# The last three units' rows by products with 0/1 matrices, and the last normed tile from its features

## The chip, the cores and the metric

The kernel runs on one core of a Trainium2 chip. The metric is device time in microseconds, from the first to the last instruction with what lies around it; lower is better. Five engines run their own queues: PE (TensorE, matmuls), DVE (VectorE), ACT (ScalarE), POOL (GpSimd) and SP (SyncE, which here only issues DMAs). They meet at semaphores.

## What is computed

One layer of an encoder for 512 tokens of width 1024, in float32: norm and one input projection, two branches (a chunked gated delta rule and a sliding-window attention), their gated merge, an output projection, then a hierarchical mixture of experts and a final norm. The part that the change touches most:

```python
def hierarchical_moe(h, w_rg, b_rg, w_re, b_re, w_gate, w_up, w_down):
    # top-1 group of 4, then top-2 of its 4 experts; weight = p_group * softmax(top-2 logits)
    ...
    for gi in range(N_EXPERT_GROUPS):
        e = slice(gi * EXPERTS_PER_GROUP, (gi + 1) * EXPERTS_PER_GROUP)
        act = jax.nn.silu(jnp.einsum('td,edf->tef', t, w_gate[e])) * jnp.einsum('td,edf->tef', t, w_up[e])
        out = out + jnp.einsum('tef,efd->td', act * combine[:, e, None], w_down[e])
...
x = x + hierarchical_moe(rms_norm(x, norm_ffn_w[layer]), ...)
return rms_norm(x, norm_final_w)
```

## The kernel before

Every float32 operand of a large product is split into a high part (rounded, on ACT) and a low part (the rest, on DVE), and `three` (L1582 to L1584) makes one product out of three matmuls: hi x hi, lo x hi, hi x lo. All matmuls of this kind have line 1582, 1583 or 1584.

**Start.** Four tiles of x (128 tokens each) are squared and rooted on ACT, scaled on DVE (L1046, L1047) and turned on PE into features (L1594). Ahead of that stands a turn of the small vectors (`small_rows`, 65 of them, L1588), which DVE copies to `small_cols` (L1041) before it scales x. The input projection follows, and in it a product for beta and decay with 8 columns of weights, 24 matmuls, and its turn (L1610).

**Routing.** After the output projection the residual sum y is turned, 20 router logits per token come from `residual_logits` (L1907), and DVE works out each token's group, its two experts (L1409 to L1444) and its place in the expert's list. Meanwhile the rows of the FFN input are written to HBM (`ffn_rows`, L598): tiles 0 to 2 normed by DVE, tile 3 scaled by ACT (L968) and multiplied by the norm's weights by POOL (L718). While PE waits it repeats a product 20 times (`keep_busy`, L1943) ahead of the rank product (L1949).

**Experts.** A unit is one expert with up to 128 of its tokens. There are 23: the 16 experts and 7 extra units for experts with more tokens, in the order of `SEQ`; numbers 4, 7, 10, 13, 16, 19 and 21 are extra ones. Their weights are gathered by POOL with computed row numbers (L703); those of the others are loaded by SP (L588). For unit u POOL gathers the tokens' rows (`fetch`, L688), PE turns them (L1983), makes gate and up, turns the hidden values (L1999) and multiplies them by the down weights; ACT copies the result to `unit_out` (L988), and POOL scatters it to `expert_rows_hbm` (`spread`, L711). Each engine writes its own loop by hand; in pass u DVE does in this order: hidden of u-1, low part of the gate weights of u+1, of the tokens of u+1 (`unit_in_lo`, L1501), of the down weights of u-1 (L1351), of the hidden values of u-1 (L1547), of the up weights of u+1. PE does in pass u: turns of u+1, first half of gate/up of u, turn of hidden u-1, second half, down of u-1.

**Tail.** When the last rows are in HBM, SP loads two rows per token back (`expert_rows`, L611), DVE adds them to y with the weights of the two choices (L1561, L1562), ACT squares and roots, DVE norms (L1568, L1569), SP stores each tile.

## Time and profile before

| | |
|---|---|
| time, median of 3 runs (lowest, highest) | 700.14 us (698.49, 701.82) |
| the profiled execution: time / span | 698.2 us / 696.5 us |
| PE busy | 644.4 us, 93% of the span |
| DVE busy | 473.3 us, 68% |
| ACT busy | 394.0 us, 57% |
| POOL busy | 176.3 us, 25% |
| chain of work that ended last, by engine | PE 83%, DVE 7%, DMA 3% |

The table gives shares over the whole. In most of the span PE is the engine that works without a pause, and the others wait for it; at the two ends and in the routing it is the other way round. So what an edit is worth has to be read at its place, from the timeline there: which engine idles in front of an instruction, and what released it.

### The profile page before, as it was taken

How to read it: one execution, taken by the hardware profiler on the slowest of the kernel's cores; microseconds unless marked ns; L12 is line 12 of the kernel's file. 1: busy time of each engine (PE TensorE's matmuls, PEld its weight loads, DVE VectorE, ACT ScalarE, POOL GpSimd, SP SyncE). 2: the span in 40 equal slices, each digit the busy share in tenths (PEclk: the TensorE clock that was granted, in tenths of full speed). 3: DMA queues.
4: the chain of work that ended last, by engine and by line, in shares of the span. 5: the costliest groups of instructions: out<-in, count | busy, mean ns of one | idle time of the engine just before them, and what ended most of it. 6: DMA issues, size and time to landing. Idle time of an engine off the chain costs nothing.

```text
span 696.5 us, 9239 instructions
## 1 busy us (share of the span) xinstructions
PE 644.4 (93%) x3371; PEld 535.8 (77%) x3372; DVE 473.3 (68%) x779; ACT 394.0 (57%) x664; POOL 176.3 (25%) x217
## 2 busy tenths in 40 slices
PE   5999999999999999999999998899999999999910
PEld 4688788788878888888888885788878888887810
DVE  4778995265521434425665549899999999998717
ACT  6449583355624233243432443388898898987623
POOL 7000009981000000000000002145545546455210
PEclk9999999999999999999999997699999999999975
DMA  8524343213222222113235615468787797866335
GB/s 270 178 67 96 61 106 121 62 60 76 66 61 62 61 61 60 62 61 95 88 121 223 260 62 191 164 196 287 216 272 249 224 313 240 292 225 216 104 140 241
DMA packets 73729, 104.63 MB, mean 150 GB/s; under 512 B 31634, under 2 KB 53203, under 8 KB 73555
## 3 DMA queue, kind: packets, MB, share of 16 engines
q1 hardware_dynamic: 60912, 95.57, 42.3%
q0 software_dynamic: 12672, 8.43, 4.0%
q8 instruction: 27, 0.44, 0.3%
q14 instruction: 20, 0.16, 0.1%
q10 hardware_dynamic: 98, 0.03, 0.0%
HBM read 123.90 MB, written 17.83 MB: 203 GB/s over the span
## 4 chain that ended last, share of the span: by engine, by line
PE 83%; DVE 7%; DMA 3%; ACT 2%; POOL 2%; issue 2%; SPq 0%; POOLq 0%; ACTq 0%; DVEq 0%
PE bank L1582 22%; PE bank L1584 22%; PE bank L1583 22%; PE bank L1983 2%; PE bank L1718 2%; PE bank L1907 1%; PE bank L1628 1%; DVE down_lo L1351 1%; DMA expert_rows<-expert_rows_hbm 1%; PE bank L1787 1%; PE bank L1777 1%; PE bank L1737 1%; DMA ew_raw<-in_w_down,extra_weight_rows 1%; PE bank L1750 1%; DVE rank_onehot L1466 1%
## 5 line engine op out<-in xcount | busy, mean ns | idle before, releaser
L1582 PE MATMUL bank<-h_hi,w_hi 128*128 128x512 f32 x304 | 123.1, 405 | 1.0 <-POOL index_row_i L662 1.0
L1584 PE MATMUL bank<-h_hi,w_lo 128*128 128x512 f32 x304 | 118.7, 390 | 0.0
L1583 PE MATMUL bank<-h_lo,w_hi 128*128 128x512 f32 x304 | 118.5, 390 | 0.0
L1351 DVE TENSOR_TENSOR gate_up_lo<-ew_raw,gate_up_hi 128x1024 fp32r<-128x1024 f32 x92 | 108.3, 1219 | 10.6 <-ACT gate_up_hi L950 8.4
L950 ACT ACTIVATE gate_up_hi<-ew_raw 128x1024 fp32r<-128x1024 f32 x92 | 92.2, 1056 | 9.1 <-DMA ew_raw<-in_w_gate,extra_weight_rows 7.8
L1037 DVE TENSOR_TENSOR w_lo<-w_raw,w_hi 128x2048 fp32r<-128x2048 f32 x26 | 60.2, 2317 | 50.1 <-ACT w_hi L744 50.0
L1582 PE MATMUL bank<-gate_up_hi,unit_in_hi 128*128 128x512 f32 x184 | 76.7, 417 | 0.0
L1584 PE MATMUL bank<-gate_up_hi,unit_in_lo 128*128 128x512 f32 x184 | 72.9, 396 | 0.0
L1583 PE MATMUL bank<-gate_up_lo,unit_in_hi 128*128 128x512 f32 x184 | 72.6, 394 | 0.0
L718 POOL TENSOR_TENSOR ffn_in_T<-ffn_in_T,norm_ffn_b 128x1024 f32<-128x1024 f32 x1 | 2.3, 2346 | 261.5 <-ACT ffn_in_T L968 261.5
L1582 PEld LDWEIGHTS bank<-h_hi,w_hi 128*128 128x128 f32 x304 | 57.2, 188 | 12.3 <-issue 1.5
L1584 PEld LDWEIGHTS bank<-h_hi,w_lo 128*128 128x128 f32 x304 | 57.1, 188 | 12.2
L1583 PEld LDWEIGHTS bank<-h_lo,w_hi 128*128 128x128 f32 x304 | 57.3, 188 | 10.5 <-issue 0.2
L744 ACT ACTIVATE w_hi<-w_raw 128x2048 fp32r<-128x2048 f32 x26 | 49.7, 1910 | 16.0 <-PE bank L1584 16.0
L1351 DVE TENSOR_TENSOR down_lo<-ew_raw,down_hi 128x1024 fp32r<-128x1024 f32 x44 | 52.0, 1222 | 6.1 <-ACT down_hi L950 4.4
L711 POOL DMA_INDIRECT expert_rows_hbm<-unit_out,row_index x23 | 25.2, 1095 | 84.3 <-DVE gate_up_lo L1351 49.7
L674 POOL TENSOR_TENSOR sub_product<-sub_low,sub_inv 128x496 f32<-128x496 f32 (+30 forms) x31 | 22.6, 730 | 89.5 <-DMA sub_low<-chunk_low_hbm 87.2
L950 ACT ACTIVATE down_hi<-ew_raw 128x1024 fp32r<-128x1024 f32 x44 | 44.5, 1072 | 0.8 <-DMA ew_raw<-in_w_down,extra_weight_rows 0.7
L1584 PEld LDWEIGHTS bank<-gate_up_hi,unit_in_lo 128*128 128x128 f32 x184 | 35.0, 190 | 7.9
L688 POOL DMA_INDIRECT unit_tokens<-ffn_rows,row_index x23 | 30.6, 1332 | 38.1 <-DVE row_index L1474 24.3
L1582 PEld LDWEIGHTS bank<-gate_up_hi,unit_in_hi 128*128 128x128 f32 x184 | 35.4, 192 | 6.0
L1583 PEld LDWEIGHTS bank<-gate_up_lo,unit_in_hi 128*128 128x128 f32 x184 | 35.2, 192 | 6.1
(361 smaller groups left out, 1335.8 us busy)
## 6 DMA issues: line engine op xcount, KB each, us to landing
w_raw<-in_w_in SPq DMA_DIRECT2D x17, 1024.0 KB, 5.2
ew_raw<-in_w_gate SPq DMA_DIRECT2D x32, 512.0 KB
ew_raw<-in_w_up SPq DMA_DIRECT2D x32, 512.0 KB
ew_raw<-in_w_down SPq DMA_DIRECT2D x32, 512.0 KB
w_raw<-in_w_out SPq DMA_DIRECT2D x4, 1024.0 KB, 5.0
expert_rows<-expert_rows_hbm SPq DMA_DIRECT2D x8, 512.0 KB, 7.3
x_T<-in_x SPq DMA_DIRECT2D x4, 512.0 KB, 4.9
w_raw<-in_w_in SPq DMA_DIRECT2D x8, 256.0 KB, 4.2
```

Source lines behind the costliest of these rows:

```text
L674: link(nc.gpsimd.tensor_tensor(sub_t[:, j + 1:, :], sub_l[:, j + 1:, j:j + 1].broadcast_to(w), sub_x[:, j:j + 1, :].broadcast_to(w), ALU.m ...
L688: nc.gpsimd.indirect_dma_start(out=xg[u % 2][:, :], out_offset=None, in_=h_rows[:, :], in_offset=bass.IndirectOffsetOnAxis(ap=ridx[:, c, 1 ...
L711: nc.gpsimd.indirect_dma_start(out=o_rows[:, :], out_offset=bass.IndirectOffsetOnAxis(ap=ridx[:, SEQ[u], 0:1], axis=0), in_=ot[u % 2][:, : ...
L744: act.activation(whi[u % RING][:, :], raw[u % RING][:, :], ACT.Copy).then_inc(hi_done, 1)
L950: act.activation(dst[half], eraw[slot][:, :], ACT.Copy).then_inc(ehi_done, 1)
L1037: dve.tensor_tensor(wlo[s][:, :], raw[s][:, :], whi[s][:, :].bitcast(F32), ALU.subtract).then_inc(lo_done, 1)
L1351: dve.tensor_tensor(dst, eraw[slot][:, :], hi.bitcast(F32), ALU.subtract).then_inc(elo_done, 1)
L1582: pe.matmul(out_ap, lhs_hi, rhs_hi, start=first, stop=False)
L1583: pe.matmul(out_ap, lhs_hi, rhs_lo, start=False, stop=False)
L1584: return pe.matmul(out_ap, lhs_lo, rhs_hi, start=False, stop=last)
L1718: ins = pe.matmul(o, qb[d, h, m * P:(m + 1) * P], kb[d, m * P - P + c0:(m + 1) * P], start=True, stop=True)
L1983: ins = pe.transpose(bank4(2 + k // 4)[:, k % 4, :], xg[u % 2][:, :].rearrange("p (c k) -> p k c", k=KT)[:, k, :], ident[:, :])
```

## The change

Six edits go in together.

1. The turns of x start before the small rows are turned; DVE copies `small_cols` after it has scaled two tiles.
2. The hi and lo weights of beta/decay stand side by side, 16 columns in one tile, and two matmuls per step (hi|lo with h_hi, hi with h_lo) replace three. The turn adds the two halves with small products.
3. The last tile of the FFN input comes from the turned residual: ACT multiplies its features by the norm's weights (`last_features`), PE turns them back (8 turns), ACT scales by the rms factor. POOL's multiply is gone. 12 repeated products stand where 20 did.
4. Unit 1's turns go to banks 5 and 4 and wait for the row numbers alone, no longer for `unit_in_lo` of unit 0.
5. The last three units (20, 21, 22; `LATE`) are not scattered to HBM. Their down product is weighted and split into hi and lo (`late_out_hi` on ACT, `late_out_lo` on DVE), and PE multiplies it by a 0/1 matrix of 128 tokens by 128 rows, per tile and unit, which adds every row to its token (`late_rows`). What is needed for it: 0/1 matrices made by DVE in pass 6 (`late_onehots`), weights of the rows, which SP writes out as a table (8 small stores) and POOL gathers in pass 12 (3 gathers of 128x1), and zeros in `expert_rows_hbm` from 16 stores early on, since rows of late units are no longer written there.
6. The rows of the other units are loaded back when unit 19 is out, and the tail adds them (`add_pair`) and the products (`add_late`) in an order written out by hand. The first add stands in DVE's pass 22, in front of the late split of unit 20.

The core of the diff:

```diff
-            dve.wait_ge(rows_ps, 1)
-            dve.tensor_copy(cols[:, :], ps[7][:, 0:65]).then_inc(cols_done, 1)
             for t in range(TT):
+                if t == 2:
+                    dve.wait_ge(rows_ps, 1)
+                    dve.tensor_copy(cols[:, :], ps[7][:, 0:65]).then_inc(cols_done, 1)
...
-                    ins = three(ps[4][0:8, :], ba_hi[:, k, :], ba_lo[:, k, :], h_hi[:, k, :], h_lo[:, k, :],
-                                k == 0, k == KT - 1)
+                    pe.matmul(ps[4][0:16, :], ba_hl[:, k, :], h_hi[:, k, :], start=k == 0, stop=False)
+                    ins = pe.matmul(ps[4][0:8, :], ba_hi[:, k, :], h_lo[:, k, :], start=False, stop=k == KT - 1)
...
+                if 4 <= u < 8:
+                    for r_ in range(2 * (u - 4), 2 * (u - 4) + 2):
+                        for half in range(2):
+                            sp.dma_start(o_rows[P * r_:P * (r_ + 1), S * half:S * (half + 1)],
+                                         sub_t[:, :, :].rearrange("p i c -> p (i c)")).then_inc(zero_rows, 16)
...
-            pool.wait_ge(choice_exp, ROW_SCALED)
-            pool.wait_ge(x2_in, 80)
-            nc.gpsimd.tensor_tensor(tx[:, TT - 1, :], tx[:, TT - 1, :], nffn[:, :], ALU.mult).then_inc(pool_set, 1)
...
+            pe.wait_ge(hf_act, TT + 1)
+            for k in range(KT):
+                ins = pe.transpose(bank4(2 + k // 4)[:, k % 4, :], last_f[:, k, :], ident[:, :])
+            ins.then_inc(tt_ps, 1)
-            keep_busy(20)
+            keep_busy(12)
...
-                if u:
+                if u == 1:
+                    pe.wait_ge(ids_done, 4)
+                elif u:
                     pe.wait_ge(xs_lo_done, u)
...
-                spread(u)
+                if u < LATE[0]:
+                    spread(u)
+                if u == 12:
+                    pool.wait_ge(wt_out, 16 * 2 * TT)
+                    pool.wait_ge(ids_done, EARLY + 4)
+                    for i, v in enumerate(LATE):
+                        nc.gpsimd.indirect_dma_start(
+                            out=l_w[:, i:i + 1], out_offset=None, in_=wt_rows[:, :],
+                            in_offset=bass.IndirectOffsetOnAxis(ap=ridx[:, SEQ[v], 0:1], axis=0),
+                            bounds_check=2 * S - 1, oob_is_err=False).then_inc(wt_in, 16)
...
-            sp.wait_ge(ot_out[(UNITS - 2) % 2], 16 * ((UNITS - 2) // 2 + 1))
-            sp.wait_ge(ot_out[(UNITS - 1) % 2], 16 * ((UNITS - 1) // 2 + 1))
-            sp.wait_ge(gu_ps, UNITS)
+            for i in range(2):
+                u = LATE[0] - 1 - i
+                sp.wait_ge(ot_out[u % 2], 16 * (u // 2 + 1))
...
+            def late_out_lo(i):
+                dve.wait_ge(xt_ps, (UNITS - 1, UNITS, UNITS)[i])
+                for h in range(2):
+                    hs = slice(S * h, S * (h + 1))
+                    dve.wait_ge(late_hi, 2 * i + h + 1)
+                    dve.scalar_tensor_tensor(l_lo[i][:, hs], ps[down_banks(LATE[i])[h]][:, :], l_w[:, i:i + 1],
+                                             l_hi[i][:, hs].bitcast(F32), ALU.mult, ALU.subtract).then_inc(late_lo, 1)
...
+                if u == UNITS - 1:
+                    add_pair(0, 0)
+                    late_out_lo(0)
+                if u == UNITS:
+                    add_pair(0, 1)
...
+                if u == 6:
+                    late_onehots()
...
+            def late_rows(t, i):
+                pe.wait_ge(late_lo, 2 * i + 2)
+                for n_ in range(2):
+                    ns = slice(S * n_, S * (n_ + 1))
+                    o = ps[late_bank[t][n_]][:, :]
+                    pe.matmul(o, l_oh[i][:, t, :], l_hi[i][:, ns], start=i == 0, stop=False)
+                    ins = pe.matmul(o, l_oh[i][:, t, :], l_lo[i][:, ns], start=False, stop=i == 2)
...
             hidden_f(UNITS - 1)
+            pe.wait_ge(late_set, 1)
+            late_rows(0, 0)
             down(UNITS - 1)
+            late_rows(0, 1)
+            late_rows(1, 0)
+            late_rows(0, 2)
+            late_rows(1, 1)
+            late_rows(1, 2)
+            for t in range(2, TT):
+                for i in range(3):
+                    late_rows(t, i)
```

Where instructions move (line numbers of the changed kernel are its own):

PE between the last router logits and the rank product, before:

```order
L1907 MATMUL bank<-router_raw,residual_F_139 128x20 x8
L1943 MATMUL bank<-index_row_repeated,earlier_tokens_b 128x512 x20
L1949 MATMUL bank<-chosen_b,earlier_tokens_b 128x64
L1952 MATMUL bank<-chosen_b,ones_b 128x16 x6
L1954 MATMUL bank<-chosen_b,ones_b 128x16 x4
```

and now:

```order
L2041 MATMUL bank<-router_raw,residual_F_137 128x20 x8
L2075 MATMUL bank<-ident,last_rows_F 128x128 x8
L2081 MATMUL bank<-index_row_repeated,earlier_tokens_b 128x512 x12
L2087 MATMUL bank<-chosen_b,earlier_tokens_b 128x64
L2090 MATMUL bank<-chosen_b,ones_b 128x16 x6
L2092 MATMUL bank<-chosen_b,ones_b 128x16 x4
```

The 8 turns of `last_rows_F` stand where 8 of the repeated products stood.

DVE in pass 6, now (before, the split of the down weights followed `unit_in_lo` at once):

```order
L1577 TENSOR_TENSOR unit_in_lo_147<-bank,unit_in_hi_145 128x512 x2
L1606 CAST index_row_f<-index_row_i 128x128
L1608 CAST late_rows<-row_index 128x1 x3
L1611 TENSOR_SCALAR late_rows_by_tile<-late_rows 128x3 x4
L1614 TENSOR_TENSOR late_onehot_264<-index_row_f,late_rows_by_tile 128x512
L1614 TENSOR_TENSOR late_onehot_265<-index_row_f,late_rows_by_tile 128x512
L1614 TENSOR_TENSOR late_onehot_266<-index_row_f,late_rows_by_tile 128x512
L1427 TENSOR_TENSOR down_lo<-ew_raw_119,down_hi 128x1024
L1427 TENSOR_TENSOR down_lo<-ew_raw_120,down_hi 128x1024
```

POOL in pass 12, before (the store of unit 12, then the gate weights of extra unit 16):

```order
L688 DMA unit_tokens_141<-ffn_rows,row_index 128x1024
L711 DMA expert_rows_hbm<-unit_out_143,row_index 1024x1024
L703 DMA ew_raw_125<-in_w_gate,extra_weight_rows 128x1024
L703 DMA ew_raw_126<-in_w_gate,extra_weight_rows 128x1024
L703 DMA ew_raw_121<-in_w_up,extra_weight_rows 128x1024
```

and now:

```order
L730 DMA unit_tokens_140<-ffn_rows,row_index 128x1024
L753 DMA expert_rows_hbm<-unit_out_142,row_index 1024x1024
L770 DMA late_weights<-slot_weights_hbm,row_index 128x1 x3
L745 DMA ew_raw_123<-in_w_gate,extra_weight_rows 128x1024
L745 DMA ew_raw_124<-in_w_gate,extra_weight_rows 128x1024
L745 DMA ew_raw_119<-in_w_up,extra_weight_rows 128x1024
```

Three gathers now stand between that store and the gate weights.

DVE from hidden 21 on, before:

```order
L1536 TENSOR_TENSOR hidden_T_151<-gate_silu,bank 128x256
L1351 TENSOR_TENSOR down_lo<-ew_raw_127,down_hi 128x1024
L1351 TENSOR_TENSOR down_lo<-ew_raw_128,down_hi 128x1024
L1547 TENSOR_TENSOR hidden_lo<-bank,hidden_hi 128x256
L1351 TENSOR_TENSOR down_lo_last<-ew_raw_121,down_hi_last 128x1024
L1351 TENSOR_TENSOR down_lo_last<-ew_raw_122,down_hi_last 128x1024
L1536 TENSOR_TENSOR hidden_T_150<-gate_silu,bank 128x256
L1547 TENSOR_TENSOR hidden_lo<-bank,hidden_hi 128x256
L1561 SCALAR_TENSOR_TENSOR y_T<-expert_rows_156,first_weight,y_T 128x1024
L1562 SCALAR_TENSOR_TENSOR y_T<-expert_rows_157,second_weight,y_T 128x1024
```

and now (`expert_rows_0` and `_1` are the rows of the two choices):

```order
L1639 TENSOR_TENSOR hidden_T_150<-gate_silu,bank 128x256
L1629 SCALAR_TENSOR_TENSOR y_T<-expert_rows_0_272,first_weight,y_T 128x1024
L1623 SCALAR_TENSOR_TENSOR late_out_lo_160<-bank,late_weights,late_out_hi_157 128x512 x2
L1427 TENSOR_TENSOR down_lo<-ew_raw_125,down_hi 128x1024
L1427 TENSOR_TENSOR down_lo<-ew_raw_126,down_hi 128x1024
L1657 TENSOR_TENSOR hidden_lo<-bank,hidden_hi 128x256
L1427 TENSOR_TENSOR down_lo_last<-ew_raw_119,down_hi_last 128x1024
L1427 TENSOR_TENSOR down_lo_last<-ew_raw_120,down_hi_last 128x1024
L1639 TENSOR_TENSOR hidden_T_149<-gate_silu,bank 128x256
L1629 SCALAR_TENSOR_TENSOR y_T<-expert_rows_1_273,second_weight,y_T 128x1024
L1657 TENSOR_TENSOR hidden_lo<-bank,hidden_hi 128x256
L1623 SCALAR_TENSOR_TENSOR late_out_lo_161<-bank,late_weights,late_out_hi_158 128x512 x2
```

One add and the late split of unit 20 now stand ahead of the split of down 21, and another add ahead of the last `hidden_lo`.

## Rows read from the trace of the kernel before

**Rows 1.** The page, busy time of PE (us, share, instructions).

```profile
PE 644.4 (93%) x3371; PEld 535.8 (77%) x3372; DVE 473.3 (68%) x779; ACT 394.0 (57%) x664; POOL 176.3 (25%) x217
```

**Rows 2.** Timeline of the start: start us, us, engine, line, work, [idle before <-releaser].

```profile
5.57 0.29 ACT L756 ACTIVATE rms_factor<-sum_squares,eps 128x1 f32<-128x1 f32 x1
...
6.42 0.34 PE L1588 MATMUL bank<-ident,small_rows 65*128 65x65 f32 x1 [6.42 <-DMA small_rows<-in_norm_ffn_w]
...
14.23 5.36 DVE L1054 SCALAR_TENSOR_TENSOR h_lo<-bank,small_cols,h_hi 128x512 fp32r<-128x512 f32 x8 [0.38 <-ACT h_hi L763]
```

**Rows 3.** Timeline of PE, the first and the last of the 24 beta/decay matmuls.

```profile
26.35 0.39 PE L1582 MATMUL bank<-h_hi,ba_hi 128*8 128x512 f32 x1
...
31.66 0.39 PE L1584 MATMUL bank<-h_hi,ba_lo 128*8 128x512 f32 x1
```

**Rows 4.** Timelines in the routing; the last row is a window with the granted clock (0.50).

```profile
421.46 2.35 POOL L718 TENSOR_TENSOR ffn_in_T<-ffn_in_T,norm_ffn_b 128x1024 f32<-128x1024 f32 x1 [261.47 <-ACT ffn_in_T L968]
...
421.50 2.33 DVE L1409 TENSOR_TENSOR group_key<-router_logits,group_max 128x16 f32<-128x16 f32 x1
423.87 0.17 DVE L1410 TENSOR_TENSOR group_key<-group_key,index_priority 128x16 f32<-128x16 f32 x1
...
420.60 6.93 PE L1943 MATMUL bank<-index_row_repeated,earlier_tokens_b 128*128 128x512 bf16 x19 [0.22 <-issue]
427.90 0.20 PE L1949 MATMUL bank<-chosen_b,earlier_tokens_b 128*128 128x64 bf16 x1 [0.37 <-DVE chosen_b L1441]
...
423.00:425.00 2.00, 2.00 (x6) 0.73 (x5) 1.83 (x6) 0.00 (x0) 0.80 (x1) 0.50 0.19 78
```

**Rows 5.** Timelines around the first unit: unit 1's turns, the extra units' one-hot, its codes.

```profile
440.73 1.95 PE L1983 MATMUL bank<-ident,unit_tokens 128*128 128x128 f32 x8 [2.34 <-DVE unit_in_lo L1501]
...
448.91 1.23 DVE L1466 TENSOR_TENSOR rank_onehot<-index_row_repeated,extra_rank 128x2048 bf16<-128x2048 bf16 x1
...
450.73 1.10 PE L1969 MATMUL bank<-extra_token_codes,rank_onehot 128*128 128x3 bf16 x16
```

**Rows 6.** Timeline of PE, first matmul of down 5; groups of DVE, the residual's add.

```profile
507.88 0.47 PE L1582 MATMUL bank<-down_hi,hidden_hi 128*128 128x512 f32 x1 [0.53 <-DVE down_lo L1351]
...
L1372 DVE TENSOR_TENSOR y_T<-y_T,bank 128x512 f32<-128x512 f32 x8 | 5.3, 685 | 7.3 <-PE bank L1584 7.3
```

**Rows 7.** Timelines of POOL, ACT, DVE and PE from unit 16's gather to down 14.

```profile
579.70 1.94 POOL L703 DMA_INDIRECT ew_raw<-in_w_gate,extra_weight_rows  x1 [0.31 <-issue]
...
584.63 2.01 ACT L950 ACTIVATE gate_up_hi<-ew_raw 128x1024 fp32r<-128x1024 f32 x2 [1.16 <-DMA ew_raw<-in_w_gate,extra_weight_rows]
...
591.84 0.41 DVE L1547 TENSOR_TENSOR hidden_lo<-bank,hidden_hi 128x256 fp32r<-128x256 f32 x1
...
592.36 0.47 PE L1582 MATMUL bank<-down_hi,hidden_hi 128*128 128x512 f32 x1
```

**Rows 8.** Timelines of the tail, and the tile's answer on how long the loads take.

```profile
645.90 0.99 POOL L711 DMA_INDIRECT expert_rows_hbm<-unit_out,row_index  x1 [7.37 <-ACT unit_out L988]
...
655.27 2.36 DVE L1351 TENSOR_TENSOR down_lo<-ew_raw,down_hi 128x1024 fp32r<-128x1024 f32 x2 [2.87 <-ACT down_hi L950]
...
663.04 0.42 DVE L1547 TENSOR_TENSOR hidden_lo<-bank,hidden_hi 128x256 fp32r<-128x256 f32 x1 [2.47 <-ACT hidden_hi L1008]
...
668.45 0.98 POOL L711 DMA_INDIRECT expert_rows_hbm<-unit_out,row_index  x1 [3.92 <-ACT unit_out L988]
...
671.70 4.87 SPq L611 DMA_DIRECT2D expert_rows<-expert_rows_hbm x8
...
676.61 1.28 DVE L1561 SCALAR_TENSOR_TENSOR y_T<-expert_rows,first_weight,y_T 128x1024 f32<-128x1024 f32 x1 [13.15 <-DMA expert_rows<-expert_rows_hbm]
...
DMA to landing us min/median/max: 3.6/7.3/9.2
...
690.43 1.06 ACT L1020 ACTIVATE square_junk<-y_T 128x1024 f32<-128x1024 f32 x1 [2.43 <-DVE y_T L1562]
...
692.14 1.29 DVE L1569 SCALAR_TENSOR_TENSOR out_T<-y_T,rms_factor,norm_final_b 128x1024 f32<-128x1024 f32 x1
```

More of the change, by code:

```diff
@@ L285, in build @@
         brg = new("router_bias", [P, NG + NE])
+        l_oh = [at(f"late_onehot{i}", [P, TT, P], F32R, r_tmp + 2048 * i) for i in range(2)]
+        l_oh.append(new("late_onehot2", [P, TT, P], F32R))
+        l_row, l_col, l_w = new("late_rows", [P, 3]), new("late_rows_by_tile", [P, 3, TT]), new("late_weights", [P, 3])
         row_rep = at("index_row_repeated", [P, P, 16], BF16, tri_at)
@@ L625, in link @@
                 pool.wait_ge(pool_step, n[0])
+            link(nc.gpsimd.memset(l_w[:, :], 0.0))
             link(nc.gpsimd.memset(ident[:, :], 0.0))
@@ L958, in _, with last_features @@
                 act.activation(hf[0][:, :, t * P:(t + 1) * P], bank4(4 + t % 3), ACT.Copy).then_inc(hf_act, 1)
+            def last_features(half):
+                for k in range(4):
+                    ins = act.activation(last_f[:, 4 * half + k, :], hf[half][:, k, S - P:], ACT.Copy,
+                                         scale=cols[:, 57 + 4 * half + k:58 + 4 * half + k])
+                return ins
             act.wait_ge(lo_done, split_count(UNITS_PRE - 1))
+            act.wait_ge(hf_act, TT)
+            last_features(0)
             for t in range(TT):
@@ L989, in unit_out, with late_out_hi @@
                 ins.then_inc(ot_done, 1)
+            def late_out_hi(i):
+                u = LATE[i]
+                act.wait_ge(dn_ps, u + 1)
+                act.wait_ge(wt_in, 48)
+                if i < 2:
+                    act.wait_ge(ot_out[u % 2], 16 * (u // 2))
+                for h in range(2):
+                    act.activation(l_hi[i][:, S * h:S * (h + 1)], ps[down_banks(u)[h]][:, :], ACT.Copy,
+                                   scale=l_w[:, i:i + 1]).then_inc(late_hi, 1)
             split_in_hi(0)
@@ L1570, in final_norm @@
                                          ALU.mult, ALU.mult).then_inc(fin_done, 1)
-            add_experts(0)
-            for t in range(1, TT):
-                add_experts(t)
-                final_norm(t - 1)
-            final_norm(TT - 1)
+            late_out_lo(1)
+            add_pair(1, 0)
+            add_pair(1, 1)
+            late_out_lo(2)
+            add_pair(2, 0)
+            add_late(0)
+            add_pair(2, 1)
+            add_late(1)
+            final_norm(0)
+            add_pair(3, 0)
+            add_late(2)
+            final_norm(1)
+            add_pair(3, 1)
+            add_late(3)
+            final_norm(2)
+            final_norm(3)
         @block.tensor
```

130 lines of the change are left out of this document (99 added, 31 removed).

## The prediction

> **What bounds the kernel now.** I read the page first: TensorE (PE) is busy for 644.4 us, 93% of the 696.5 us span [rows 1]. In such a kernel an edit pays in three ways: it takes matmuls off PE where PE never waits, it shortens a wait of PE, or it shortens the two ends where PE has nothing to do. So the views that count are the timelines at the places where the change cuts in: the start [rows 2], the small beta/decay product [rows 3], the routing between output projection and experts [rows 4, 5], two places inside the expert loop [rows 6, 7], and the tail [rows 8]. The tail is largest: the last hidden_lo starts at 663.04 and lasts 0.42, then DVE idles until the rows come back from HBM at 676.61, and the last out_T ends at 692.14 + 1.29 = 693.43, which leaves 3.07 us for its store [rows 8]. From the end of hidden_lo (663.46) to the end there are 33.0 us.
>
> **Base of the sum.** The profiled execution has a span of 696.5 us and a time of 698.2; the median of the three runs is 700.14, which is 1.9 above it. I make the sum on the span and carry the difference over to the median.
>
> **1. Start (transposes of x ahead of the small rows).** Today DVE stands still until the small rows have landed (PE 6.42, after a wait of 6.42) and been turned and copied, while the first rms factor was ready at 5.57 + 0.29 = 5.86 [rows 2]. Now x is scaled from 5.9 on, so PE's first turns come about 1.1 us earlier, less 0.34 for the small-rows turn that now stands between them: 0.7. But the first h_lo has only 0.38 us of idle time before it; what is next in line is DVE's own w_lo ahead of it. So the gain is 0.38, with 0 and 0.7 as bounds. **-0.4.**
>
> **2. Beta/decay product.** The 24 narrow matmuls start at 26.35 and the last at 31.66, 0.231 us apart [rows 3]; they have 8 columns of weights and still take the time of 512 streamed columns. Joined hi|lo leaves 16, so 8 x 0.231 = 1.85 goes, while 4 tiny turns become 8 small products of 8 columns (0.1 each is my estimate: the 4 old ones are a small fraction of these rows). PE has no wait anywhere near, so this is all path: **-1.6** (bounds -1.8 and -1.2).
>
> **3. Zero rows.** 16 stores of 256 KB are queued on SP behind the w_raw loads of units 4 to 7. These loads are about 11 us apart in PE's pace (48 matmuls of 0.23), the stores are 1 MB per load, and nobody waits for them but POOL, which idles then. Nothing; if that cover fails, the next load slips by the 2 to 3 us of its zero stores.
>
> **4. Routing.** POOL's multiply runs 421.46 to 423.81; DVE's first group_key, 16 elements wide, starts at 421.50 and takes 2.33 us, where its neighbour takes 0.17 [rows 4]. So the multiply holds DVE up; that chain is the critical one up to the row indices. With the multiply gone the chain is 2.16 shorter. The Trainium skill's page SBUF — State Buffer (Reading the diagram) says the same: a two-input DVE instruction and a GpSimd instruction that reads SBUF take turns at one port pair, whole instructions at a time. By that page the stall goes with the multiply; the trace agrees.
> What is next late is PE: 20 repeated products start at 420.60 and 19 recorded ones last 6.93, and the rank product waits just 0.37 for DVE [rows 4]. Now 8 turns and 12 products stand there. PE is at 1.2 GHz (granted 0.5, [rows 4]); 8 turns cost 1.95 as in [rows 5], so the turns end at 422.4, and 12 products at about 0.43 end between 426.8 and 427.5, where DVE is ready at 427.9 - 2.2 = 425.7. The rank product thus starts 0.4 to 1.1 us earlier, not 2.2; DVE's slack before it needs the ranks gives a little back. I take 1.2 (bounds 0.5 and 2.1).
> Then unit 1's turns: today PE waits 2.34 us for unit_in_lo 0 and turns after it (1.95) [rows 5]. In other banks the turns fill that wait, so gate_up 0 starts 1.95 earlier. But the extra units' first one-hot on DVE (448.91, 1.23 long, so done at 450.14) gates the row codes ahead of gate_up 1, which start at 450.73 today [rows 5]. DVE gains the 1.2 and, as unit 1's turns are now there before it asks, about half a us of idle time (estimate): the one-hot is done at 448.4 and the codes follow at once, 2.3 earlier than today. So PE's 3.1 at gate_up 0 shrinks to **-2.3** for the whole stage (bounds -1.2 and -4.0).
>
> **5. One-hots for the late rows, in unit 6.** Six kinds of work on DVE: a cast, small copies, four small scalars (about 0.9 together), and three two-source operations of 512 columns, for which I take the residual's add, eight of which are 5.3 us busy, 0.66 each less the overlap of neighbours, 0.6 [rows 6]. Together 2.7. They stand right ahead of the split of down 5, and PE's down 5 at 507.88 already waits 0.53 for that split [rows 6]. No slack exists at this point, and later units are PE-bound, so it is not given back: **+2.7** (bounds 0, if another queue holds down 5 anyway, and 3.0).
>
> **6. Three gathers of weights, in unit 12.** They go into POOL's queue between the store of unit 12 and the gate gather of extra unit 16, issued at 579.70 after a pause of 0.31 [rows 7]. An indirect transfer takes 0.98 at the least (668.45 in [rows 8]) and with the pause 1.3; three are 3.9. ACT already waits 1.16 us for that gather before 584.63, and the chain ACT, DVE, down 14 ends in PE at 592.36 with hidden_lo 14 at 591.84 + 0.41 just before it [rows 7]: no slack. So **+3.8** (bounds 0.5, if the small ones take next to no POOL time, and 4.2). The eight small stores on SP before unit 5's loads cost nothing: SP waits for free slots there.
>
> **7. Unit 22 on DVE.** Between hidden 21 and the split of down 21 DVE idles 2.87 us, until 655.27 [rows 8]. There now stand one add of expert rows (1.28 in [rows 8], 1.32 with its link) and late_out_lo 0 (eight of the h_lo kind take 5.36 in [rows 2], so 1.35 for two): 2.67. But the add waits for its rows. Store of unit 19: POOL 645.90, and the like of it went from 668.45 to SP's first load at 671.70, 3.25 us; so loads from 649.2. The first pair took 4.9 us (671.70 to 676.61), the loads have 3.6/7.3/9.2 as min, median and max [rows 8]. I take a landing at 655.0, a little later than 654.1 for the weight gather still running. DVE then reaches the split 2.3 us late; 0.8 is slack on PE's side, 0.4 is won back since ACT no longer copies unit 21 ahead of hidden 22. **+1.1** (bounds -0.7, rows there by 652.7, and +4.5, landing after 9.2).
>
> **8. Tail.** After hidden_lo 22 DVE has: late_out_lo 1 and 2 (2.7), six adds of rows (7.9), four adds of the late products (two 512-column operations from PSUM each, the like of the residual's add in [rows 6], so 1.3 each: 5.2), two norms (2.8), and then add, square, root and norm of the last tile: from the square's start at 690.43 to the last out_T's end 3.0 today [rows 8], the same now. That is 21.6, with the store 24.7, against 33.0: **-8.3**. PE's 36 products after down 22 at 0.23 (8.3 us) stay ahead of DVE: the last tile's are done some 3 us before DVE asks for them. The removed wait (10 us of stores, loads and queue) is hidden behind DVE's own list. At 1.2 GHz they would take 0.43 each and the end would be 3.5 later; since PE never stops for more than 2 us here, I don't expect it. Bounds -9 and -4.8.
>
> **Sum.** -0.4 - 1.6 - 2.3 + 2.7 + 3.8 + 1.1 - 8.3 = -5.0. Span 691.5, on the median **695.1 us**, 0.7% faster.
>
> **Rivals.**
> A. *The helpers are hidden.* The one-hots or the gathers cost nothing, because PE is not really held at down 5 or down 14. For: in this trace PE's two waits are 0.53 and about 0.1 us, near zero, and the loop's DMA timing may move. Against: both stand in queues with no idle time behind them. One hidden: 692 or 691; both: 688.6. Chance 0.27.
> B. *The gain in routing and tail is smaller.* The rank product waits for PE's repeated products (0.5 instead of 1.2), the late products run at 1.2 GHz (+3.5) or the pair lands late (+2): 697 to 699. For: the clock is at 0.5 all through routing. Chance 0.20.
> C. *Slower.* DVE stops in unit 22 in front of its first add, with the splits of down 21 and 22 queued behind it, so a late pair of rows stops PE as well. Every us of landing after 655 is a us on the end. Up to the old time it would have to land at 660, 10.8 us after issue; the slowest load in the trace took 9.2, though without a weight gather beside it. At 664 the time is 704. Chance 0.06.
>
> **How the numbers follow.** My forecast (691.5 to 697.5 on the median, both helpers paid) has 0.47, A 0.27, B 0.20, C 0.06. The measurement can tell about 0.5% (3.5 us) from no change, so faster means below 696.6. From the forecast 0.38 lies below it, from A 0.27, from B 0.05: faster 0.70. Slower needs over 703.6: 0.05 with C; the rest, 0.25, is the same. The range leaves 1 in 10 of A below and C with the worst of B above: 689.0 to 699.0.
>
> **What would show it.** In the profile after: the first h_lo at 13.9; 16 narrow matmuls; group_key at 0.2 us and the rank product waiting for PE; gate_up 0 about 3 us earlier, gate_up 1 about 2; PE idle 3 us before down 5 and nearly 4 before down 14; DVE idle in unit 22 up to 655 (less the shift); 25 us from the last hidden_lo to the end. I am wrong if PE shows no such idle at down 5 and down 14 (A), or if the late products take 0.43 us each or DVE waits for late_rows (B).

## The result and the profile after

| | before | after |
|---|---|---|
| median of 4 runs (lowest, highest) | 699.32 us (697.18, 701.82) | 712.79 us (711.95, 713.97) |
| the profiled execution: time / span | 698.2 / 696.5 us | 712.25 / 710.5 us |

The ratio is 1.0194, with a 95% interval of 1.0170 to 1.0219: the changed kernel is 1.9% slower, where 0.7% faster was forecast. On the span it is 14.0 us more, where 5.0 less was forecast.

PE's row of the page answers [rows 1]:

```profile
PE 659.2 (93%) x3423; PEld 549.6 (77%) x3424; DVE 483.5 (68%) x804; ACT 397.1 (56%) x673; POOL 171.8 (24%) x217
```

14.8 us more of busy time and 14.0 us more of span, so PE idles about as long as before: it waits less at the two ends and in the routing, and longer in between. Of the busy time 11 us are the 48 late products (0.23 each). A ledger shows where the time goes: for each unit, the start of its down product after minus its start before ("down 2" is the down product of unit 2). Each entry is the difference of two rows of PE's timelines; where it changes, something happened. "Half clock" stands for a granted clock of 0.50 (1.2 GHz), at which matmuls of 512 columns follow each other every 0.43 us; at the full clock it is 0.23.

| place | after - before, us | step |
|---|---|---|
| first product after beta/decay (31.5) | -0.4 | start +1.48, 24 products now 16: -1.84 |
| projections from 44 on, up to the router logits | +1.1 | turn of beta/decay +1.5 |
| down 0 | -1.3 | routing and first units -2.4 |
| down 1 | -1.4 | |
| down 2 | +8.9 | **wait of PE +10.3** |
| down 3, 4 | +11.6 | down 2 at half clock +2.7 |
| down 5 to 13 | +13.1 | 0/1 matrices +1.5 |
| down 14 | +18.2 | **gathers of weights +5.1** |
| down 15 to 18 | +20.8 | down 14 at half clock +2.5 |
| down 19, 20 | +20.4 | 0.4 come back |
| down 21 | +23.1 | unit 22 +2.7 |
| last hidden_lo | +22.5 | |
| end | +14.0 | tail -8.5 |

**The large item is the first.** Four timelines, of SP, POOL, ACT and PE (start us, us, engine, line, work, what ended the idle time before it), and the tile's answer on how long the small stores take:

```profile
462.10 1.85 SPq L635 DMA_DIRECT2D slot_weights_hbm<-first_weight  x4
464.00 2.57 SPq L635 DMA_DIRECT2D slot_weights_hbm<-second_weight  x4
...
DMA to landing us min/median/max: 2.2/9.0/13.8
...
462.89 2.05 POOL L745 DMA_INDIRECT ew_raw<-in_w_gate,extra_weight_rows  x1 [0.30 <-issue]
465.24 1.00 POOL L745 DMA_INDIRECT ew_raw<-in_w_gate,extra_weight_rows  x1 [0.30 <-DVE down_lo L1427]
...
479.81 2.00 ACT L998 ACTIVATE gate_up_hi<-ew_raw 128x1024 fp32r<-128x1024 f32 x2 [12.42 <-DMA ew_raw<-in_w_gate,extra_weight_rows]
...
487.53 0.77 PE L1704 MATMUL bank<-down_hi,hidden_hi 128*128 128x512 f32 x1 [10.19 <-DVE hidden_lo L1657]
488.09 0.63 PE L1705 MATMUL bank<-down_lo,hidden_hi 128*128 128x512 f32 x1
```

The eight stores write 4 KB in all and take up to 13.8 us (the 2.2 is one of the three gathers that read the table later; the stores alone take 6.0 to 13.8). The gate weights of extra unit 4, gathered just behind them, let ACT wait 12.42 us; ACT's split of them stands ahead of everything that down 2 needs, so PE waits 10.19. Then its matmuls follow each other every 0.43 us in place of 0.23. Before, ACT waited 0.47 us for the same weights and down 2 started at 478.62 without a wait:

```profile
469.28 2.01 ACT L950 ACTIVATE gate_up_hi<-ew_raw 128x1024 fp32r<-128x1024 f32 x2 [0.47 <-DMA ew_raw<-in_w_gate,extra_weight_rows]
```

The chain of waits after names the gather:

```profile
465.24 14.49 DMA ew_raw<-in_w_gate,extra_weight_rows
```

What the queues did meanwhile is in the windows (the last two numbers are the share of the DMA engines' time and GB/s; the one ahead of them is the granted clock). Before, after, and the window after the wait:

```profile
468.00:478.00 10.00, 10.00 (x62) 8.54 (x61) 9.93 (x14) 8.19 (x12) 6.48 (x5) 1.00 0.74 236
...
468.00:478.00 10.00, 9.34 (x58) 7.69 (x56) 1.75 (x4) 0.00 (x0) 2.04 (x2) 1.00 0.95 95
...
480.00:490.00 10.00, 2.47 (x6) 2.02 (x7) 8.85 (x12) 9.97 (x14) 2.95 (x2) 0.50 0.66 202
```

The DMA engines are busier (0.95 against 0.74) and move less (95 GB/s against 236). That the writes are to blame isn't to be read from this view; the experiments below test it. ACT does nothing for ten us, and in the window in which PE's wait ends the granted clock is 0.50 (1.2 GHz).

**The other places**, after:

```profile
15.25 0.77 PE L1704 MATMUL bank<-h_hi,w_hi 128*128 128x512 f32 x1 [2.28 <-DVE h_lo L1130]
...
42.50 1.95 PE L1743 MATMUL bank<-ident,ba_F 16*128 16x8 f32 x16
...
426.53 0.20 PE L2087 MATMUL bank<-chosen_b,earlier_tokens_b 128*128 128x64 bf16 x1
...
448.24 1.15 PE L2107 MATMUL bank<-extra_token_codes,rank_onehot 128*128 128x3 bf16 x16 [2.30 <-DVE rank_onehot L1542]
449.25 0.77 PE L1704 MATMUL bank<-gate_up_hi,unit_in_hi 128*128 128x512 f32 x1
...
516.39 1.90 DVE L1614 TENSOR_TENSOR late_onehot<-index_row_f,late_rows_by_tile 128x512 fp32r<-128x512 f32 x3
520.99 0.47 PE L1704 MATMUL bank<-down_hi,hidden_hi 128*128 128x512 f32 x1 [2.01 <-DVE down_lo L1427]
...
596.83 1.00 POOL L745 DMA_INDIRECT ew_raw<-in_w_gate,extra_weight_rows  x1 [0.30 <-issue]
602.82 2.01 ACT L998 ACTIVATE gate_up_hi<-ew_raw 128x1024 fp32r<-128x1024 f32 x2 [6.36 <-DMA ew_raw<-in_w_gate,extra_weight_rows]
610.54 0.77 PE L1704 MATMUL bank<-down_hi,hidden_hi 128*128 128x512 f32 x1 [5.05 <-DVE hidden_lo L1657]
...
676.40 1.28 DVE L1629 SCALAR_TENSOR_TENSOR y_T<-expert_rows,first_weight,y_T 128x1024 f32<-128x1024 f32 x1 [3.50 <-DMA expert_rows<-expert_rows_hbm]
681.83 0.47 PE L1704 MATMUL bank<-down_hi,hidden_hi 128*128 128x512 f32 x1 [2.55 <-DVE hidden_lo L1657]
685.56 0.42 DVE L1657 TENSOR_TENSOR hidden_lo<-bank,hidden_hi 128x256 fp32r<-128x256 f32 x1
...
693.97 0.40 PE L2181 MATMUL bank<-late_out_hi,late_onehot 128*128 128x512 f32 x1
694.21 0.39 PE L2182 MATMUL bank<-late_out_lo,late_onehot 128*128 128x512 f32 x1
...
706.21 1.28 DVE L1680 SCALAR_TENSOR_TENSOR out_T<-y_T,rms_factor,norm_final_b 128x1024 f32<-128x1024 f32 x1
```

They answer [rows 2] to [rows 8] in order and are read point by point below. For the first of them the row before, at the same product, was:

```profile
15.13 0.47 PE L1582 MATMUL bank<-h_hi,w_hi 128*128 128x512 f32 x1 [1.03 <-POOL index_row_i L662]
```

The releaser is inferred, and a POOL instruction happened to end just then; what the product waits for is the first h_lo, behind whose start it comes 0.90 us before (14.23 [rows 2]) and 0.89 after (14.36), where h_lo is named. The tail is as foreseen: from the end of the last hidden_lo (685.98) to the end of the span are 24.5 us, against 33.0 [rows 8].

### The profile page after: what moved, and what is told of

It is laid out like the page before. It is cut to its first block, busy times and chain, and to the rows that moved or that the text cites. A ratio compares the mean times of both kernels' runs of the same rounds, so it can differ in the third digit from the quotient of the medians.

```text
span 710.5 us, 9413 instructions
## 1 busy us (share of the span) xinstructions
PE 659.2 (93%) x3423; PEld 549.6 (77%) x3424; DVE 483.5 (68%) x804; ACT 397.1 (56%) x673; POOL 171.8 (24%) x217
## 4 chain that ended last, share of the span: by engine, by line
PE 71%; DVE 13%; DMA 7%; ACT 4%; issue 3%; POOL 1%; SPq 0%; POOLq 0%; ACTq 0%; DVEq 0%
PE bank L1704 19%; PE bank L1706 18%; PE bank L1705 18%; DMA ew_raw<-in_w_gate,extra_weight_rows 3%; DVE down_lo L1427 3%; PE bank L1852 2%; DMA w_raw<-in_w_in 1%; DVE gate_up_lo L1427 1%; PE bank L2123 1%; DVE y_T L1629 1%; DVE rank_onehot L1542 1%; PE bank L1762 1%; POOL ew_raw L745 1%; ACT gate_up_hi L998 1%; PE bank L1921 1%
## 5 line engine op out<-in xcount | busy, mean ns | idle before, releaser
L1704 PE MATMUL bank<-down_hi,hidden_hi 128*128 128x512 f32 x88 | 36.9, 419 | 20.9 <-DVE hidden_lo L1657 17.8
L753 POOL DMA_INDIRECT expert_rows_hbm<-unit_out,row_index x20 | 20.6, 1031 | 89.9 <-ACT unit_out L1050 45.7
```

Source lines behind the costliest of these rows:

```text
L753: nc.gpsimd.indirect_dma_start(out=o_rows[:, :], out_offset=bass.IndirectOffsetOnAxis(ap=ridx[:, SEQ[u], 0:1], axis=0), in_=ot[u % 2][:, : ...
L1704: pe.matmul(out_ap, lhs_hi, rhs_hi, start=first, stop=False)
```

## The experiments

Every ratio is to the kernel before, run beside it on the same chip. "-9 against after" compares a median with 712.8, which was not measured beside it; nor were x13, x16, x17 and x18 beside x10_order22, with which they are compared. The kernel before had medians of 699.3 to 699.8 each time. Where a kernel is a repaired one, all repairs are named.

### Are the stores the cause?

**x1_stores_alone**: the kernel before, with only this added.

```diff
             for u in range(1, UNITS - 1):
+                if u == 4:
+                    sp.wait_ge(ids_done, EARLY)
+                    for k, w in enumerate((w1, w2)):
+                        for t in range(TT):
+                            r0 = S * k + P * t
+                            sp.dma_start(wt_rows[r0:r0 + P, :], w[:, t:t + 1]).then_inc(wt_out, 16)
```

> The kernel before with one thing added: the 8 stores of the slot weights on SP ahead of unit 5's loads, 1024 rows of 4 bytes; nothing reads them. Theory T (the 4-byte writes hold the DMA queues, and everything issued behind them lands late): PE stops for about 10 us in front of down 2 and does part of it at half clock, so about 13 us more than the kernel before, near 712. Rival R (the writes are harmless; the stall of the changed kernel comes from SP's place in the order, from the zero rows or from the three gathers): 699 to 701, no stall at down 2. If only the 4.4 us that SP spends on issuing them counts, it is hidden too: 699 to 701.

Measured 706.1 against 699.6, ratio 1.0098 (1.0066 to 1.0130): the stores alone cost 6.5 us, not nothing, and not 13. The trace, POOL, SP, ACT and PE:

```profile
464.57 1.02 POOL L712 DMA_INDIRECT ew_raw<-in_w_gate,extra_weight_rows  x1 [0.31 <-DVE gate_up_lo L1360]
...
464.91 2.37 SPq L607 DMA_DIRECT2D slot_weights_hbm<-first_weight  x4
...
474.84 2.01 ACT L959 ACTIVATE gate_up_hi<-ew_raw 128x1024 fp32r<-128x1024 f32 x2 [5.45 <-DMA ew_raw<-in_w_gate,extra_weight_rows]
...
482.57 0.47 PE L1591 MATMUL bank<-down_hi,hidden_hi 128*128 128x512 f32 x1 [3.22 <-DVE down_lo L1360]
...
468.00:478.00 10.00, 10.00 (x62) 8.57 (x61) 6.45 (x9) 4.08 (x7) 2.98 (x3) 1.00 0.66 87
```

The same stall, less deep: 87 GB/s in the window, ACT's wait 5.45 in place of 12.42, PE's 3.22 in place of 10.19, with no lower clock behind it. Here the first gate gather left 0.3 us before the stores; in the changed kernel they were 0.8 us ahead of it. That this order makes the difference fits the two traces and was not tried by itself.

**x3_row_stores**: the changed kernel, the table written as 8 rows of 512 bytes (PE turns the 128x8 weights, DVE copies), in one store that stands two passes later, ahead of unit 7's loads. So the number of stores and their place change together with the size of the rows; x15_table_apart below changes the layout alone.

```diff
-                            sp.dma_start(wt_rows[r0:r0 + P, :], w[:, t:t + 1]).then_inc(wt_out, 16)
+                    sp.dma_start(wt_rows[:, :].rearrange("(r p) o -> r (p o)", p=P), wt_t[:, :]).then_inc(wt_out, 16)
```

> The changed kernel, with the same table written otherwise: PE turns the 8 columns of weights into 8 rows of 128, DVE copies them, and SP writes 8 rows of 512 bytes in one store ahead of unit 7's loads. Theory T: the 13.0 us of the first stall are gone, 713 - 13 = 700, and PE's wait at down 2 is under 1 us. Rival R: 711 to 714, the stall stays.

703.8, ratio 1.0049 (1.0026 to 1.0071): -9.0 against after. The stall at down 2 is gone from the ledger (down 1 and 2 both -2.4). Not all 13 us come back, because later waits grow: its ledger rises by 3.8 us over downs 4 to 6 and by 4.4 from down 18 to down 21, the changed kernel's by 1.4 and 2.4. That the stall had given the loads time there fits, and was not tried by itself.

### What in the stores is dear?

Four kernels, all the kernel before with 8 stores of 1024 rows in all at the same place; the size of a row and its distance in HBM differ. x12 writes the weights, as x1 does; the other three take their rows from the identity matrix.

> The kernel before with 8 stores at the same place and of as many rows (1024), but each row has 512 bytes (the identity matrix as the source). If it is the number of rows that holds the queues, the loss is that of the 4-byte rows, about 13 us (712). If it is that a row has 4 bytes only, the 512 KB take about 2 to 3 us of the queues, little of which reaches PE: 699 to 702, and the gathers of extra unit 4 land in under 8 us.

> The kernel before with 8 stores of 1024 rows in all, of 64 bytes each (16 columns of the identity matrix), where x1_stores_alone had 4 bytes and x2_stores_512 had 512. If every row shorter than 512 bytes holds the queues in the same way, the loss is that of the 4-byte rows, 6 us (706). If the loss goes with the size of the element, 64 bytes are nearer to the 512-byte rows: 700 to 702.

> The kernel before with the same 8 stores of 4-byte elements as x1_stores_alone, but into a table whose rows are 64 bytes apart, so that no two elements are neighbours in HBM. If the loss comes from 16 elements sharing each 64-byte piece of HBM (x9_stores_64, with a piece per row, lost nothing): no loss, 699 to 701. If it comes from the element being 4 bytes: the loss of x1_stores_alone, 705 to 708.

> The kernel before with 8 stores of 1024 rows of 16 bytes each, one right behind the other in HBM, so four share a piece of 64 bytes. If neighbours that share a piece are the cause, a loss between none and that of x1_stores_alone, 1 to 5 us (701 to 705). If only the element of 4 bytes is dear: 699 to 701.

| rows | ratio to before (95%) | GB/s, 468 to 478 us | PE's wait at down 2, us |
|---|---|---|---|
| none (the kernel before) | | 236 | 0 |
| 4 bytes, neighbours (x1) | 1.0098 (1.0066 to 1.0130) | 87 | 3.22 |
| 4 bytes, 64 apart (x12) | 1.0008 (0.9986 to 1.0031) | 203 | 1.53 |
| 16 bytes, neighbours (x14) | 1.0014 (0.9988 to 1.0041) | 198 | 1.01 |
| 64 bytes (x9) | 1.0009 (0.9987 to 1.0030) | 237 | 0.29 |
| 512 bytes (x2) | 1.0011 (0.9985 to 1.0036) | 285 | 0 |

The last two columns are from one profile each. The windows behind the GB/s, x12 and then x9:

```profile
468.00:478.00 10.00, 10.00 (x63) 8.53 (x61) 7.80 (x11) 6.21 (x10) 4.77 (x5) 1.00 0.75 203
...
468.00:478.00 10.00, 10.00 (x62) 8.38 (x60) 9.09 (x13) 7.50 (x12) 5.99 (x5) 1.00 0.83 237
```

In the time neither the number of rows nor the 4 bytes are dear: the same 1024 elements, 64 bytes apart, cost nothing that the time can show, though their stores came 0.8 us ahead of the gathers (463.77, 464.56), as in the changed kernel. Dear is that sixteen of them are neighbours within 64 bytes. The profiles show a smaller effect besides: the smaller the rows, the longer PE waits at down 2, up to 1.53 us with 4 bytes 64 apart. Part of that may reach the time, since the intervals leave room for 0.3 to 0.4% (2 to 3 us). Why neighbours are slow no run shows.

The Trainium skill's page DMA: Bandwidth & Descriptors (Specifications) says that line rate wants 512 bytes and more, and that below it the DMA does read-modify-write. By that rule every row here but the 512-byte ones loses something. The waits at down 2 go that way (0.29 with 64 bytes, 1.01 with 16, 1.53 with 4 apart), but only the 4-byte neighbours cost time beyond the interval, so the measurement decides: the rule is a reason to be suspicious of small writes and doesn't say which ones stop a kernel.

**x15_table_apart**: the changed kernel, each weight repeated 16 times by DVE (two more copies) so that a row has 64 bytes, which the three gathers then fetch.

```diff
-                            sp.dma_start(wt_rows[r0:r0 + P, :], w[:, t:t + 1]).then_inc(wt_out, 16)
+                            sp.dma_start(wt_rows[r0:r0 + P, :], w16[:, k, t, :]).then_inc(wt_out, 16)
```

> The changed kernel with one difference: each weight is repeated 16 times, so that the 8 stores write 1024 rows of 64 bytes and no two tokens share a piece of 64 bytes; number, place and order of the stores are those of the changed kernel. If neighbours in HBM are the cause: as x3_row_stores, 703 to 705. If it is the number of rows or SP's place: 711 to 714.

704.9, ratio 1.0091 (1.0071 to 1.0110): -7.9 against after, with as many stores at the same place. PE's wait at down 2 is 0.30 in place of 10.19, so the neighbours are the cause of the first stall in the changed kernel too. Part of the 13 us is lost again at down 5, where the ledger rises by 5.6 (a wait of 3.31 and half clock) and the changed kernel's by 1.5.

**x11_stores_late**: the changed kernel with its stores five passes later (`if u == 9:`).

> The changed kernel with its 8 small stores as they are, but five passes later on SP, ahead of unit 10's loads, where the gate weights of extra unit 10 are gathered too. If the writes hold everything behind them wherever they stand: PE waits at down 6 to 9 in place of down 2, and the time stays within 3 us of the changed kernel, 710 to 714. If the loss was due to the place alone (they came 0.8 us ahead of the gathers of extra unit 4, with no load in reserve yet): 700 to 703.

708.3, ratio 1.0125 (1.0095 to 1.0155), between the two: -4.5 against after. PE waits 3.3 us at down 7 and does part of it at half clock; the ledger gives 5.2 us there (and 4.3 at down 5, as in the other kernels without the first stall). So the writes cost at both places, and about 8 us more at the first, where gathers are queued right behind them and no load that landed earlier is in reserve. That this is the reason for the 8 us fits and was not tried by itself.

### The gathers and the 0/1 matrices

**x4_gathers_13**: the changed kernel with `if u == 13:` for the three gathers.

> The changed kernel with the three gathers of weights in POOL's pass 13 and not 12, so that no gather of an extra unit's weights is queued right behind them. Theory Q (they cost by POOL's queue alone: the gate gather of extra unit 16 starts 3.9 us later, PE waits 5.1 us at down 14 and does what follows at half clock): 7.6 us less than the changed kernel, 705. Rival (the gathers of 4-byte elements hold the DMA queues as the stores do, wherever they stand): under 3 us less, 710 to 713, and PE waits at down 15 or 16 instead.

703.9, ratio 1.0058 (1.0033 to 1.0084): -8.9 against after, and the ledger is flat at down 14 (+11.8, then +12.2). **x17_gathers_12** is the reverse of it in a kernel without the first stall: x10_order22, below, with the gathers back in pass 12.

> x10_order22 with the three gathers of weights back in POOL's pass 12, ahead of the gate gathers of extra unit 16. If they cost by POOL's queue and by the clock that PE loses after its wait: 5 to 7.6 us more than x10_order22, 694 to 696.5, with a wait of 4 to 5 us at down 14. If that cost hung on the first stall: 689 to 691.

695.8 against 688.8 for x10_order22, so 7.0 us. Its trace, ACT and PE at down 14:

```profile
586.68 2.01 ACT L999 ACTIVATE gate_up_hi<-ew_raw 128x1024 fp32r<-128x1024 f32 x2 [6.48 <-DMA ew_raw<-in_w_gate,extra_weight_rows]
...
594.41 0.76 PE L1708 MATMUL bank<-down_hi,hidden_hi 128*128 128x512 f32 x1 [5.27 <-DVE hidden_lo L1657]
```

The 3.9 us on POOL's queue become 5.3 us of PE's wait and 2 of half clock; it doesn't hang on the first stall.

**x7_onehots_late**: the changed kernel with `late_onehots()` in pass 22 in place of 6. **x18_onehots_6**: x10_order22 with it back in pass 6.

> The changed kernel with the 0/1 matrices made in pass 22, where DVE stood idle 3.5 us for the expert rows, in place of pass 6. Theory (no slack in pass 6, free in pass 22): the 1.5 us of PE's wait at down 5 are gone and nothing comes back, 711.3. Rival (pass 22 isn't free either, since the rows land at once): 712 to 713, the wait only moved from down 5 to down 21.

> x10_order22 with the 0/1 matrices back in DVE's pass 6. In pass 22 they cost DVE 2.8 us where it had idle time; in pass 6 PE waits for the split behind them. Theory: 1.5 to 2.7 us more at down 5, less 1 us that DVE then has at the end: 689 to 691. Rival: nothing is left of it at the end, since pass 22 then gains all of it back: 688 to 689.

For x7, 708.4 (ratio 1.0142, 1.0102 to 1.0182) is -4.4 against after, more than the 1.5 expected; but its ledger differs from the changed kernel's already at the first stall (+5.6 at down 2, against +8.9), so it is no clean price of the matrices. x18 has 691.7 (ratio 0.9882, 0.9865 to 0.9899) against 688.8 (0.9851, 0.9824 to 0.9878) for x10_order22: 2.9 us, just above the 689 to 691 of its theory, but the two intervals overlap and the difference is barely clear of the noise. The mechanism is in the profile (which is of the slowest of its five runs): the ledger rises by 4.0 us over downs 5 and 6. Its PE at down 5, and the sixth matmul after that:

```profile
507.19 0.47 PE L1709 MATMUL bank<-down_hi,hidden_hi 128*128 128x512 f32 x1 [2.89 <-DVE down_lo L1429]
...
508.73 0.63 PE L1709 MATMUL bank<-down_hi,hidden_hi 128*128 128x512 f32 x1
```

The wait is 2.89 (0.35 in x10_order22), and the clock falls behind it, too.

### The repairs together

**x8_joined**: the changed kernel with rows of 512 bytes, gathers in pass 13, the old start, 4 turns and an add on DVE for beta/decay, and the matrices in pass 22. The diff shows the turns.

```diff
-                    for q in range(2):
-                        ins = pe.matmul(ps[5][:, 8 * t:8 * t + 8], ba_f[:, t * P:(t + 1) * P], ident[0:16, 8 * q:8 * q + 8],
-                                        start=q == 0, stop=q == 1)
+                    ins = pe.transpose(ps[5][:, 16 * t:16 * t + 16], ba_f[:, t * P:(t + 1) * P], ident[0:16, 0:16])
```

> The changed kernel with five repairs at once: the table written in rows of 512 bytes, its gathers in POOL's pass 13, the start as in the kernel before, the 16 columns of beta/decay turned by 4 turns and added on DVE in place of the small products, and the 0/1 matrices made in DVE's idle time of pass 22 in place of pass 6. If the terms read from the trace add up, the sum against the kernel before is: beta/decay -1.8, routing -2.2, waits for the extra units' late weights +2.0, unit 22 +2.0, tail -8.5, so -8.5 and about 691 (ratio 0.988). Rival (what is freed goes into the waits for loads, since PE then runs ahead of the DMA queues): -4 or less, 695 to 700.

**x10_order22** moves DVE's first add of expert rows from pass 22 into pass 23, and the second behind the loop; **x13_joined_start** is x10_order22 with the start of the changed kernel; **x16_joined_apart** is x10_order22 with the table in rows of 64 bytes.

> The same as x8_joined, but DVE's first add of expert rows stands in pass 23, behind the low parts of down 21 and 22, so that DVE doesn't wait for the rows with these queued behind. If that wait holds up the end: 1 to 2 us less than x8_joined, and the wait of PE at down 21 is under 1 us. Rival (the down weights of unit 21 land that late themselves): no difference.

> x10_order22 with the start as in the changed kernel (the turns of x ahead of the small rows). In the traces so far the small rows landed at 8.0 to 8.3 us in every kernel with the change, and the first beta/decay product started at 28.0 with the old order of the start, at 26.4 and 26.7 with the new one where PE kept its clock, at 27.8 and 28.2 where it fell. Theory: up to 1.6 less than x10_order22, 687.2 to 688.8, if the clock is kept. Rival: the same within 0.3, since the clock falls in half of the runs.

> x10_order22 with the table in rows of 64 bytes by 8 stores ahead of unit 5's loads, in place of PE's turn and one store of 8 rows. Theory: the same time, 688 to 690.5. Rival: the 64-byte rows still delay the gate weights of extra unit 4 (ACT waited 2.5 us for them in x9_stores_64, 0.5 in the kernel before); here the routing is done 2 us earlier, so there is less cover, and 2 to 4 us come back, 691 to 693.

| kernel | median, us | ratio to before (95%) |
|---|---|---|
| x8_joined | 689.2 | 0.9843 (0.9814 to 0.9873) |
| x10_order22 | 688.8 | 0.9851 (0.9824 to 0.9878) |
| x13_joined_start | 690.0 | 0.9857 (0.9833 to 0.9881) |
| x16_joined_apart | 690.1 | 0.9877 (0.9852 to 0.9902) |

x8_joined beats both kernels, the one before by 10.1 us (1.6%) where its sum said 8.5, and the changed one by 23.6. The other three can't be told from it. In x10_order22 PE's wait at down 21 (1.67 in x8_joined) is gone and the profiled span is 1.1 less, but the medians differ by 0.4, so the 1 to 2 us that it was to bring are not shown. In x13_joined_start the earlier turns only make PE wait longer for the first h_lo (it comes 0.89 us behind that one's start at 14.48 here too, whatever POOL row is named) and start at half clock, as in the changed kernel:

```profile
15.37 0.76 PE L1709 MATMUL bank<-h_hi,w_hi 128*128 128x512 f32 x1 [2.25 <-POOL index_row_i L704]
```

For x16_joined_apart the rival has something: ACT waits 2.9 us for the gate weights of extra unit 4, and the ledger loses 1.1 us there.

## Why the prediction was wrong

The step that failed is the last sentence of step 6: "The eight small stores on SP before unit 5's loads cost nothing: SP waits for free slots there." It priced what SP does to issue them (4.4 us, indeed hidden) and not what 1024 neighbouring 4-byte writes do to the DMA queues that everybody shares. Measured: 13.0 us in the changed kernel (10.3 of wait, 2.7 of half clock), 6.5 alone, 7.9 given back when the layout of the table changes at the same place. The trace before has no write of such small pieces; the bound from both sides that an unknown cost needs was missing here, and with it the rival.

- **Start, forecast -0.4, measured +1.5.** PE turned x 1.2 us earlier (6.75, before 7.98), but the first h_lo came at 14.36, not at 13.9 (before 14.23): ACT's first w_hi started at 12.12, before at 11.54, since its weights landed later. So PE waited 2.28 us for h_lo, where it had waited 1.03, and the first seven products of h ran at 1.2 GHz. That PE may come out of a longer wait at half clock was not in the step. It isn't a steady loss: of six other profiles with this start PE kept its clock in two (x4, x7) and lost it in four (x3, x11, x13, x15).
- **Beta/decay, -1.6, measured -0.4.** 16 products for 24 give -1.84, as said. The "8 small products of 8 columns (0.1 each)" are 16 records and take 1.95 us, against 0.4 for the 4 turns. The term of the turn was mis-sized by 1.2; x8_joined, with 4 turns, takes 0.42.
- **Zero rows, 0.** Right: nothing in the ledger from 44 us to the router logits.
- **Routing, -2.3, measured -2.4**, but not by its parts, so the hit is partly luck. group_key takes 0.17 as foreseen. The rank product comes 2.4 us earlier relative to the router logits, not 1.2: it does wait for PE's repeated products, but 11 recorded ones take 3.39 us, 0.31 each, so they didn't all run at the 0.43 that the step gave them. The codes come 3.6 us earlier relative to the router logits. Of this 1.3 are lost again, since PE has waited 2.30 us for the one-hot and the next six matmuls run at half clock.
- **0/1 matrices, +2.7**: DVE's part takes 2.66 us (515.55 to 518.21), as foreseen. PE's wait at down 5 is 2.01 against 0.53, so +1.5 in the changed kernel. In x11, x15 and x18, which have no stall ahead of it, the ledger rises by 4.0 to 5.6 there, with the half clock that the step left out; that the first stall hid part of the cost fits this. The mechanism was right, rival A wrong.
- **Gathers, +3.8, measured +7.6** (7.0 in isolation). POOL issued the gather 4.1 us later than the ledger's 13.0 give, near the 3.9 foreseen; ACT started on it 5.99 us after its issue, where it had been 4.93, which makes PE's wait 5.05. The other 2.5 are the half clock of down 14, which the step left out.
- **Unit 22, +1.1, measured +2.1.** The rows landed 10.0 us after unit 19's store was issued (666.39 to 676.40), not 9.1, as the loads came 4.7 us behind the store. Rival C's mechanism is there, with 2 us, and is not what made the kernel slower.
- **Tail, -8.3, measured -8.5.** Right in size and cause: DVE has no idle time over 0.2 us from 676 on, and PE's late products stand 0.23 us apart.

With these sizes in place of mine (+1.9 start, +1.2 beta/decay, -0.1 routing, -1.2 matrices, +3.8 gathers, +1.0 unit 22, -0.2 tail) the forecast of -5.0 becomes +1.4, and the stores add 13.0; the 14.4 are the ledger's 14.0 but for 0.4 that came back at down 19. So the stores are most of the loss and not all of the error: without them the changed kernel is still no faster, as x3_row_stores (+0.5%) and x15_table_apart (+0.9%) show. Rival B looked for the lower clock in the late products; it sat in what follows new waits of PE. The reason of step 8 for a full clock in the tail ("PE never stops for more than 2 us here") doesn't hold: PE stopped for 2.55 us at down 21 and the late products still ran at full clock, while in x13, x17 and x18 they lost it for 7 or 8 products after a wait of 2.0.

## What to carry to other kernels

A DMA is priced by what it does to the queues that others use, not by the time its engine takes to issue it; a table of single numbers is written as rows (turn it first) or spread out, and neither packed 4 bytes by 4 bytes nor put right ahead of a gather with no load in reserve. A wait that an edit gives to TensorE is priced together with the matmuls behind it, which may run at half clock (up to 2.7 us for one down product here). Helpers of a new scheme (gathers, 0/1 matrices) go into a pass in which their queue has nothing urgent behind them: the same three gathers cost 7 us in pass 12 and 0.4 at down 14 in pass 13 (x4).

## What the runs showed of the hardware

- 1024 writes of 4 bytes to neighbouring addresses took up to 13.8 us to land and left 87 to 95 GB/s where 236 was moved otherwise; 64 bytes apart they left 203 GB/s, a wait of PE of 1.53 us in the profile, and no cost that the time could show.
- The length of a wait doesn't tell by itself whether TensorE comes out of it at full clock. At down products it did after 2.01 (after, x4), 2.20 (x13), 2.27 (x8), 2.54 (x15), 2.55 (after) and 3.22 us (x1), and fell to half clock within the next six matmuls after 1.87 (x7), 2.17 and 2.38 (x3), 2.28 (x11), 2.45 (x4), 2.74 (x14), 2.89 (x18), 3.27 and 3.34 (x11). After 3.31 (x15) and after each wait of 4.48 to 10.19 us the first matmul ran at 1.2 GHz already, and 8 to all 12 matmuls of the down product ran so. Waits of 2.00 and 2.01 us ahead of the late products were followed by full clock in x10 and x16 and by half clock in x13, x17 and x18. At the start, 2.28 (after), 2.25 (x13) and 2.38 (x11) were followed by half clock at once, 2.44 (x3) and 2.46 (x15) four or five matmuls later, and 2.45 (x4) and 2.50 (x7) not at all. Two rows of x1 and two of x7:

```profile
482.57 0.47 PE L1591 MATMUL bank<-down_hi,hidden_hi 128*128 128x512 f32 x1 [3.22 <-DVE down_lo L1360]
482.88 0.39 PE L1592 MATMUL bank<-down_lo,hidden_hi 128*128 128x512 f32 x1
...
655.80 0.53 PE L1703 MATMUL bank<-down_hi,hidden_hi 128*128 128x512 f32 x1 [1.87 <-DVE down_lo L1427]
656.13 0.63 PE L1704 MATMUL bank<-down_lo,hidden_hi 128*128 128x512 f32 x1
```

- A product in plain float32 is two records here: 8 small ones of 8 columns with 16 columns of weights took 1.95 us in all, where 4 turns of 16 columns took 0.42.
